# Which engine computes the low parts of the attention weights, split by tile width

## The reference, cut to what matters

```
sc = einsum('bghtd,bgtkld->bghtkl', q, k) * scale       # scores, float32
p  = softmax(where(valid, sc, MASK_VALUE))
o  = einsum('bghtkl,bgtkld->bghtd', p, v)               # one such pair for each branch
o_attn = g3[..., 0:1] * o_cmp + g3[..., 1:2] * o_slc + g3[..., 2:3] * o_win
o_attn = o_attn.reshape(b, s_len, ATTN_WIDTH) * silu(z_attn)
```

## Time and profile before

| | us |
|---|---|
| median of three runs | 957.96 |
| the profiled execution | 959.54 |
| its span, from the first to the last instruction | 957.7 |
| PE busy | 901.0 (94%) |
| DVE busy | 511.5 (53%) |
| ACT busy | 393.7 (41%) |
| POOL busy | 215.9 (23%) |

### The profile page before, as it was taken

One profiled execution on the slowest core, in us unless ns is written; L12 is line 12 of the kernel. 1 busy time (PEld: TensorE's weight loads), 2 busy tenths in 40 slices (PEclk: granted clock), 3 DMA queues, 4 the chain that ended last, 5 costly groups with the idle time before them and its releaser, 6 DMA issues.

```text
span 957.7 us, 14379 instructions
## 1 busy us (share of the span) xinstructions
PE 901.0 (94%) x5573; PEld 737.8 (77%) x5581; DVE 511.5 (53%) x1079; ACT 393.7 (41%) x789; POOL 215.9 (23%) x213
## 2 busy tenths in 40 slices
PE   0799999999999999999999999999999999999997
PEld 0478999779999876677677676788888888887885
DVE  1570355349675486886877877652232222236544
ACT  5532331522124268668677678641112111133221
POOL 6239622111000013213113122145553000000000
PEclk9989999999999999999999999999999999999999
DMA  9926033032010000000000001052332212033222
GB/s 313 356 68 131 2 70 115 1 90 47 1 45 1 1 1 1 1 2 1 1 1 1 1 2 34 14 152 61 94 105 55 61 28 61 29 147 132 89 88 88
DMA packets 53861, 59.69 MB, mean 62 GB/s; under 512 B 10113, under 2 KB 45505, under 8 KB 52753
## 3 DMA queue, kind: packets, MB, share of 16 engines
q1 hardware_dynamic: 51536, 54.13, 18.7%
q0 software_dynamic: 2000, 4.54, 1.7%
q10 hardware_dynamic: 256, 0.09, 0.0%
HBM read 52.92 MB, written 5.24 MB: 61 GB/s over the span
## 4 chain that ended last, share of the span: by engine, by line
PE 85%; ACT 4%; DVE 4%; SPq 3%; issue 2%; DMA 2%; POOL 1%; DVEq 0%; POOLq 0%; ACTq 0%
PE bank L1654 40%; PE win_max L1654 22%; PE slc_max L1654 19%; PE bank L1657 4%; SPq L507 2%; DMA ada<-in_w_ada 2%; ACT phi L836 1%; DVE rt L1182 1%; POOL qc L781 1%; ACT osb L836 0%; ACT yt L836 0%; SPq L509 0%; ACT qc L836 0%; DVE otmp L1182 0%; ACT pt L836 0%
## 5 line engine op out<-in xcount | busy, mean ns | idle before, releaser
L1182 DVE TENSOR_TENSOR plo<-pt,phi 128x512 fp32r<-128x512 f32 x192 | 105.3, 561 | 41.6 <-ACT phi L836 40.3
L836 ACT ACTIVATE pt<-bank 128x512 f32<-128x512 f32 (+1 forms) x208 | 99.8, 480 | 64.6 <-PE bank L1654 63.1
L1654 PE MATMUL bank<-q,k 128*128 128x512 f32 (+7 forms) x384 | 102.5, 348 | 0.1
L836 ACT ACTIVATE phi<-bank 128x512 fp32r<-128x512 f32 (+1 forms) x208 | 99.7, 479 | 0.0
L622 POOL TENSOR_TENSOR qa<-qa,otmp 128x256 f32<-128x256 f32 x32 | 26.1, 816 | 210.1 <-DVE otmp L1182 210.1
L1654 PEld LDWEIGHTS bank<-q,k 128*128 128x128 f32 (+1 forms) x384 | 62.8, 190 | 9.6 <-ACT phi L836 1.6
L1654 PE MATMUL bank<-phi,vhi 128*65 128x512 f32 (+3 forms) x160 | 59.4, 371 | 5.1 <-ACT osb L836 5.0
L1456 DVE TENSOR_REDUCE mx<-slc_max 128x1 f32<-128x128 f32 (+3 forms) x64 | 48.0, 750 | 8.5 <-PE slc_max L1654 8.5
L1654 PE MATMUL bank<-plo,vhi 128*65 128x512 f32 (+3 forms) x160 | 52.1, 326 | 0.0
L1654 PE MATMUL bank<-phi,vlo 128*64 128x512 f32 (+3 forms) x160 | 52.0, 325 | 0.0
L1654 PE MATMUL bank<-ht_hi,dhi 128*128 128x512 f32 x128 | 49.8, 389 | 0.0
(11 more groups left out here) (433 smaller groups left out, 2552.0 us busy)
## 6 DMA issues: line engine op xcount, KB each, us to landing
ada<-in_w_ada SPq DMA_DIRECT2D x8, 1024.0 KB, 17.2
draw<-in_w_in SPq DMA_DIRECT2D x16, 512.0 KB, 4.0
wraw<-in_w_in SPq DMA_DIRECT2D x7, 1024.0 KB, 5.3
xs<-in_x SPq DMA_DIRECT2D x8, 512.0 KB, 11.1
gstage<-in_w_ada POOLq DMA_DIRECT2D x16, 256.0 KB, 3.2
oraw<-in_w_out SPq DMA_DIRECT2D x8, 512.0 KB, 6.4
xr<-in_x SPq DMA_DIRECT2D x8, 512.0 KB, 4.1
out<-yr SPq DMA_DIRECT2D x7, 512.0 KB, 2.9
```

Source lines behind the costliest of these rows:

```text
L836: return nc.scalar.activation(o, i, fn, **kw)
L1182: return V.tensor_tensor(o, a, b, op)
L1654: return T.matmul(o, l, r, start=start, stop=stop, **kw)
```

## The change

Units of up to 256 columns get their low part from POOL, the wider ones from DVE; the compressed branch stays with POOL. A predicate `on_pool(u)` says which, and `low_no(e, pool_)` counts how many low parts the named engine has made up to unit e, for PE's waits. POOL emits its new instructions at step `S` of the unit itself, in the place where the compressed ones stood. Order and operands of all other instructions stay.

```diff
+    def on_pool(u):
+
+        br, _, _, lo, hi_ = units[u][0:5]
+        return br == 0 or hi_ - lo <= 256
+
+    def low_no(e, pool_):
+
+        h, u = divmod(e, NU)
+        mine = [on_pool(v) == pool_ for v in range(NU)]
+        return h * sum(mine) + sum(mine[:u + 1])
...
-                elif step[0] == "S" and units[step[1] % NU][0] == 0:
+                elif step[0] == "S" and on_pool(step[1] % NU):
...
-                    tt(phi[e % NPT][HD:P, :], pt[e % NPT][HD:P, :], f(phi[e % NPT][HD:P, :]), ALU.subtract)\
-                        .then_inc(once("plo_cmp"), 1)
+                    br, _, _, lo, hi_ = units[e % NU][0:5]
+                    if br == 0:
+                        tt(phi[e % NPT][HD:P, :], pt[e % NPT][HD:P, :], f(phi[e % NPT][HD:P, :]), ALU.subtract)\
+                            .then_inc(once("plo_cmp"), 1)
+                    else:
+                        tt(plo[e % NPT][:, 0:hi_ - lo], pt[e % NPT][:, 0:hi_ - lo], f(phi[e % NPT][:, 0:hi_ - lo]),
+                           ALU.subtract).then_inc(once("plo_cmp"), 1)
...
-                if br == 0:
+                if on_pool(e % NU):
                     return
                 dve.wait_ge(once("exp"), 2 * e + 2)
...
-                    if br == 0:
-                        pe.wait_ge(once("plo_cmp"), 2 * h + u + 1)
+                    if on_pool(u):
+                        pe.wait_ge(once("plo_cmp"), low_no(e, True))
                     else:
-                        pe.wait_ge(once("plo"), (NU - 2) * h + u - 1)
+                        pe.wait_ge(once("plo"), low_no(e, False))
```

## The result

The changed kernel takes 970.23 us (median of 4 runs, 969.4 to 970.9) against 958.78 us (median of 4, 957.68 to 961.02): a ratio of 1.0116, with a 95% interval of 1.0094 to 1.0138. It is slower, as forecast, but by 11.4 us and not by 5.9. The time is 6.3 us above the 963.9 us of the forecast and 0.6 us above the top of the range; 0.8 us of this is the kernel before, which measured 958.78 us beside the change and 957.96 us ahead of it. The profiled execution has a span of 968.7 us, 11.0 more than before.

What follows compares the result with a forecast made beforehand. PE, busy 94% of the span, was taken to set the pace, with DVE's relief worth 0. Delays of 4.5 + 0.6 + 0.8 = 5.9 us on 957.96 us gave 963.9 us, range 959.2 to 969.6.

Steps and rivals of the forecast that it cites:

- Step 1: End of heads 0 to 5: unit 24's low part delays POOL's copy of the queries, 6 x 0.75 = 4.5 us.
- the first of the two cases: At the query copy, DVE's `qc` instruction runs before POOL's low part, so the copy ends 0.81 us later.
- Step 2: Behind unit 5, heads 1 to 6: POOL's low part delays its product, DVE's subtraction and PE's transpose, 6 x 0.1 = 0.6 us.
- Step 3: End of the last head: POOL's low parts of units 24 and 25 come later for PE, 0.8 us.
- the alternative: Last head: DVE's `dlo` starts before POOL's low part of unit 25, and PE loads 2.5 us later.
- The locks add up: Rival: dearer low parts, small DVE products caught and the last head's race lost, 11.2 us more, 969.2 us; chance 0.15.
- Paid back: Rival: PE's waits for ACT's accumulator copies absorb the late query copy, leaving 1.4 us, 959.4 us; chance 0.19.
- The lighter DVE wins: Rival: DVE's chain at the end of a head comes 0.90 us earlier in seven heads, 951.1 us; chance 0.08.

Runs made afterwards that it cites:

- x4: Kernel before, with only the low parts of units 12, 13, 16, 17, 19 and 20 moved to POOL: 959.5 us, ratio 0.9992.
- x10: Kernel before; DVE makes unit 24's low part early, its `qc` instruction waits for POOL's query copy; units 12, 13, 16, 17, 19, 20 on POOL: 956.06 us.
- x1: Changed kernel, with the low part of unit 24 back on DVE in heads 0 to 6: 965.86 us, ratio 1.0070.
- x5: Kernel before, with only the low part of unit 24 in heads 0 to 6 moved to POOL: 964.23 us, ratio 1.0038.
- x6: Changed kernel, with POOL making unit 24's low part behind the copy of the queries in heads 0 to 5: 965.09 us, ratio 1.0066.
- x3: Changed kernel, with the low part of unit 5 back on DVE in all heads: 968.06 us, ratio 1.0094.
- x7: Changed kernel, with POOL making unit 5's low part behind its sum and product in heads 1 to 7: 969.29 us, ratio 1.0092.
- x2: Changed kernel, with units 24 and 25 of the last head alone back on DVE: 966.55 us, ratio 1.0082.

## Why the prediction was right or wrong

- **What bounds the kernel**: right. PE sets the pace, and what counted was what stands ahead of PE's waits. DVE's relief was worth 0, as booked: no V comes earlier by it anywhere in the change, and x4 and x10 show none either.
- **Price of one low part on POOL**: right for 256 columns (0.74 taken, 0.73 to 0.75 measured without a wait), and 0.46 instead of 0.53 for 128.
- **Step 1**, 4.5 us taken, 4.8 in the trace, and shown by x1, x5 and x6 from three sides. DVE was first, as in the first of the two cases (+0.81 each).
- **Step 2**, 0.6 us taken (0.1 in each of six heads), 2.8 measured: this is the first of the steps that failed. The mechanism was wrong in its order: I had DVE's subtraction waiting for POOL's product, 0.47 us on the chain to PE's transpose. In fact POOL waited for DVE, the subtraction lost nothing, and `wrow`, which the sum did without because "no row here shows" it, was caught in every such head, with 0.54 us. That the two sizes lie so near is luck. The larger part of the error is PE's room. I let PE's load follow 0.05 us behind the end of DVE's product, a figure from the copy; it follows 0.13 us behind, and a head loses 0.24 us there. And I had looked for the delay only at this transpose: DVE runs without a pause behind it, and the rest came out four units later, at a wait whose room I had not read, 0.19 us more in each head. Of the 0.33 us per head that were missing, some 0.07 are the chain, 0.08 the lag of 0.13 and 0.19 the later wait; the last head, which I had at nothing, adds 0.25. x3 shows that all of it hangs on unit 5, x7 that the two losses have different room. The range had too little as well: the step's own end was 3.0 us, and 1.5 went into it.
- **Step 3**, 0.8 us taken, 2.45 and then 1.33 more: the second step that failed. The race between POOL's low part of unit 25 and DVE's `dlo`, which I had given to POOL by 0.04 us, went to DVE by 0.14: POOL left 0.23 us between its sum and the next low part and 0.13 between the two low parts, where I had counted 0.09 and 0.08. A race within 0.04 us was not one to settle by such gaps; the alternative was in the text (+2.5, and 2.45 came). That PE's clock would fall behind such a standstill was not in the sum at all; x2 and the profile of x7 show the loss gone where the clock stays at 1.00.
- **The rivals.** "The locks add up" named two of the causes (small products caught, race lost) and gave 969.2 us; it had the chance 0.15. That its sum of 11.2 us comes so near to the 11.4 is luck: it has 3.3 us too much in step 1, for a dearer low part that did not come, 2.2 too little in step 2, and nothing for the clock's 1.3. "Paid back" is excluded: PE's waits for ACT's copies are the same to the tenth. "The lighter DVE wins" is excluded by x4 and x10, whose moved units 19 and 20 are the narrow ones ahead of the chain in question.
- **The size of the error**: 2.2 us of step 2, 1.6 of the lost race and 1.3 of the clock are 5.1 of the 5.5 us that were missing; 0.3 of step 1 are most of the rest.

## What to carry to other kernels

When work goes to an engine with time to spare, read its queue, not its busy share: 60% of the moved work cost nothing here, and 6 instructions of 80 ahead of the one copy that PE waits for cost 4.8 us. Where two engines exclude each other, list every instruction that can be caught, the tiny ones in a chain first, and take the lost side of each close race into the sum; a delay on an engine without pauses has to be followed to every later wait, not only to the next. The wait that a loss points at is also where the gain lies: freeing the same copy from the lock made the kernel before 0.3% faster.

## What the runs showed of the hardware

- A DVE product of four elements per partition takes 0.16 us, and 0.70 us when POOL's 128x256 product has started before it (six times in the change, never in the kernel before). In each pair looked at here, with two SBUF inputs on DVE's side, the later starter of the two engines waits, the smallest too, and it ends 0.03 us (this one), 0.54 us (512 columns on DVE) or 0.60 us (256 columns on POOL) behind the other's end.
- POOL's subtraction takes 0.46 us for 128 columns, 0.74 for 256 and 1.28 for 64 rows of 512, without a wait; between two instructions of POOL of which the second waits for the first there are 0.07 to 0.23 us, and two races with DVE, lost by 0.03 and 0.14 us, were decided by such gaps.
- After PE had been busy for 0.97 us of 3.00, the granted clock was 0.50 in the next 2 us and 0.72 in the 2 us behind, full again after that: 1.33 us lost. The same standstill gave a loss of 1.4 to 1.6 us in the traces of x1, x3 and x6, and none in that of x7, where the clock stayed at 1.00; each is the trace of one execution. So it may or may not fall; what decides was not tried.
